# The opening of a two-block transformer kernel: input in two transfers, a split of the first weights by VectorE, and another order of the first products

## What is computed

```
mod_l = (silu(c) @ ada_w[0] + ada_b[0])          # shifts, scales and gates
h_l = rms_norm(x_lat, norm1_g[0]) * (1 + s1_l) + sh1_l
h_c = rms_norm(x_ctx, norm1_g[0]) * (1 + s1_c) + sh1_c
h = concatenate([h_c, h_l], axis=1)
proj = h @ w_in                                   # q, k, v, r
q, k, v, r = split(proj, [512, 1024, 2048])
q, k = rope_2d(q), rope_2d(k)                     # on the latent tokens
...
```

## Time and profile before

| | |
|---|---|
| median of three runs | 2332.44 us |
| the profiled execution | 2329.71 us, span 2327.6 us |
| TensorE busy | 1946.0 us, 84% of the span |
| VectorE, ScalarE, GpSimd busy | 930.4, 687.7 and 93.8 us |
| DMA | 592.29 MB, mean 254 GB/s |
| mean granted TensorE clock | 0.938 |

### The profile page before, as it was taken

The page is one execution under the profiler, slowest core; times in us unless marked ns, Lnnn a source line. Parts: engine busy times, 40 slices in busy tenths (PEclk is TensorE's granted clock), DMA queues, the critical chain, the costliest instruction groups (busy, mean ns, idle before and its releaser), DMA issues.

```text
span 2327.6 us, 38292 instructions
## 1 busy us (share of the span) xinstructions
PE 1946.0 (84%) x16711; PEld 1467.0 (63%) x16711; DVE 930.4 (40%) x1634; ACT 687.7 (30%) x1253; POOL 93.8 (4%) x112
## 2 busy tenths in 40 slices
PE   6998899999999999999998999666666576666666
PEld 4996667888788887999896476433333343333433
DVE  4446745433524246665666365333111121111111
ACT  4334435222424246554553322111111011111111
POOL 0011110000001011000200000000000000000000
PEclk9999999999999999999999999888888888888889
DMA  6316553221225224444530359999999999999997
GB/s 277 145 37 274 199 226 131 78 109 53 97 96 217 109 74 173 177 165 150 217 121 10 157 207 397 426 427 427 427 427 427 427 426 427 427 427 427 428 427 311
DMA packets 48007, 592.29 MB, mean 254 GB/s; under 512 B 5934, under 2 KB 6890, under 8 KB 12001
## 3 DMA queue, kind: packets, MB, share of 16 engines
q1 hardware_dynamic: 44416, 580.21, 60.8%
q0 software_dynamic: 2992, 8.57, 1.2%
q10 hardware_dynamic: 432, 1.06, 0.1%
HBM read 588.77 MB, written 1.05 MB: 253 GB/s over the span
## 4 chain that ended last, share of the span: by engine, by line
PE 47%; DMA 29%; DVE 6%; ACT 4%; issue 2%; POOL 0%; SPq 0%; DVEq 0%; ACTq 0%; POOLq 0%
DMA s_ring<-in_w_up 14%; PE bank L725 10%; PE bank L727 10%; PE bank L726 10%; DMA s_arena<-in_w_up 6%; PE bank L1458 5%; DMA s_xT<-in_w_up 4%; DMA s_hT<-in_w_up 3%; DVE s_ring_r L2416 2%; ACT s_arena_r L1694 2%; PE bank L1494 2%; DMA s_xT<-in_w_down 1%; PE bank L1445 1%; PE bank L1277 1%; PE bank L1500 1%
## 5 line engine op out<-in xcount | busy, mean ns | idle before, releaser
L725 PE MATMUL bank<-s_arena_r 128*128 128x256 f32 (+2 forms) x1858 | 603.9, 325 | 8.5 <-DVE s_hT_r L2421 3.9
L727 PE MATMUL bank<-s_arena_r,s_ring_r 128*128 128x256 f32 (+2 forms) x1514 | 499.7, 330 | 0.0
L1694 ACT ACTIVATE s_arena<-bank 32x256 f32<-32x256 f32 (+6 forms) x418 | 167.9, 407 | 1001.7 <-PE bank L1458 536.9
L1458 PE MATMUL bank<-s_ring,s_arena 128*32 128x256 f32 x1952 | 281.0, 506 | 143.2 <-DMA s_hT<-in_w_up 40.3
L726 PE MATMUL bank<-s_hT_r,s_arena_r 128*128 128x512 f32 (+2 forms) x1200 | 399.3, 333 | 0.0
L725 PEld LDWEIGHTS bank<-s_arena_r 128*128 128x128 f32 x1858 | 347.9, 187 | 46.0 <-issue 8.9
L2416 DVE TENSOR_TENSOR s_ring_r<-s_ring,s_arena_r 128x2048 fp32r<-128x2048 f32 (+3 forms) x120 | 247.8, 2077 | 273.7 <-ACT s_arena_r L1694 273.6
L727 PEld LDWEIGHTS bank<-s_arena_r,s_ring_r 128*128 128x128 f32 x1514 | 284.8, 188 | 28.8
L1458 PEld LDWEIGHTS bank<-s_ring,s_arena 128*32 128x32 f32 x1952 | 136.0, 144 | 218.4 <-issue 205.8
L1694 ACT ACTIVATE s_arena_r<-s_ring 128x2048 fp32r<-128x2048 f32 (+3 forms) x120 | 206.2, 1730 | 153.5 <-PE bank L727 123.6
L726 PEld LDWEIGHTS bank<-s_hT_r,s_arena_r 128*128 128x128 f32 x1200 | 225.3, 188 | 24.1 <-issue 0.5
(11 more groups left out here) (398 smaller groups left out, 2505.2 us busy)
## 6 DMA issues: line engine op xcount, KB each, us to landing
s_ring<-in_slabs SPq DMA_DIRECT2D x68, 2048.0 KB, 8.3
s_ring<-in_w_down SPq DMA_DIRECT2D x32, 2048.0 KB, 28.9
s_ring<-in_w_up SPq DMA_DIRECT2D x31, 2048.0 KB, 33.7
s_ring<-in_w_gate SPq DMA_DIRECT2D x30, 2048.0 KB, 33.2
s_arena<-in_w_gate SPq DMA_DIRECT2D x16, 2048.0 KB, 33.5
s_arena<-in_w_up SPq DMA_DIRECT2D x16, 2048.0 KB, 33.2
s_arena<-in_w_down SPq DMA_DIRECT2D x14, 2048.0 KB, 28.8
s_ring<-in_slabs SPq DMA_DIRECT2D x16, 1408.0 KB, 6.1
```

The lines of the kernel that those rows point to most:

```text
L725: mm(out, w_hi_, x_hi_, start=start, stop=False, skip_group_check=skip)
L727: return mm(out, w_lo_, x_hi_, start=False, stop=stop, skip_group_check=skip)
L1458: last = mm(pb[b][32 * q:32 * q + 32, 0:256], x[:, c, :], (gate, up)[q // 2](c, q % 2), start=c == 0, stop=c == DC - 1, skip_group_check=True)
L1694: return act.activation(out, in_, func, **kw)
```

## The change

Six edits, all in the opening.

1. SP fetches `xT` in two transfers of four chunks. The first signals `early_in`, the second `xT_in`. `ka` now signals `early_in` too, and both TensorE (before `ada_rows(0)`) and ACT (before the first squares) wait for `early_in` at 32, that is for the first half of `xT` and for `ka`. ACT waits for `xT_in` before chunk 4.
2. GpSimd waits until `w_lo` is 1. It then rounds all of quarter 1, and after it only chunks 4 to 7 of quarter 0.
3. VectorE rounds chunks 0 to 3 of quarter 0 itself and takes their rest (`first_w_in(0, 0, 4)`). Its order is now: factors 0 to 5, columns, factors 6 and 7, rest of chunk 0, this half quarter, rests of chunks 1 and 2, quarter 1, rest of chunk 3, second half of quarter 0, columns.
4. TensorE starts with units 0 and 1 on chunks 0 to 2, then `ada_rows(2)`, chunk 3 of both, `ada_turn(2)`, unit 2 on chunks 0 to 3, `ada_rows(3)`, unit 3 on chunks 0 and 1, `ada_turn(3)`, unit 3 on chunks 2 and 3, and then chunks 4 to 7 of units 0 to 3 interleaved. The RoPE products come two by two behind units 4 to 6.
5. ACT rounds quarter 2 before it drains unit 0 rather than after unit 1.
6. `w_lo` counts one more step, so its later thresholds rise by one.

```diff
--- before.py
+++ after.py
@@ -34,8 +34,8 @@
 NE, NG, EPG = 64, 8, 8
 DE = 512
 
-W_GLA, W_FFN, W_NA = 19, FC + DC, 17
-W_GLA_OUT = 13
+W_GLA, W_FFN, W_NA = 20, FC + DC, 17
+W_GLA_OUT = 14
 W_NA_OUT = W_GLA + W_FFN + 11
 A_NA_W = 16
 H_AT = [0 * DC, 2 * DC, 3 * DC, 5 * DC, 6 * DC]
@@ -520,7 +520,8 @@
 
         @block.sync
         def _(sp):
-            sp.dma_start(xT[:, :, :], d["xT"].rearrange("p (c t) -> p c t", t=TT)).then_inc(S["xT_in"], 16)
+            for c0, sem in ((0, "early_in"), (DC // 2, "xT_in")):
+                sp.dma_start(xT[:, c0:c0 + DC // 2, :], d["xT"].rearrange("p (c t) -> p c t", t=TT)[:, c0:c0 + DC // 2, :]).then_inc(S[sem], 16)
             for n in range(len(slabs)):
                 if free[n]:
                     sp.wait_ge(S[free[n][0]], free[n][1])
@@ -620,9 +621,9 @@
             pool.memset(one1[:, :], 1.0).then_inc(S["ones_set"], 1)
             pool.memset(ada_sc, 0.0).then_inc(S["pool_set"], 1)
             pool.memset(eps[:, :], EPS).then_inc(S["ones_set"], 1)
-            pool.wait_ge(S[landed[gla_at[0]][0]], landed[gla_at[0]][1])
-            for k in range(2):
-                pool.tensor_copy(g_w_hi[k], half(place[gla_at[0]], k)).then_inc(S["pool_set"], 1)
+            pool.wait_ge(S["w_lo"], 1)
+            for k, c0 in ((1, 0), (0, DC // 2)):
+                pool.tensor_copy(g_w_hi[k][:, c0:DC, :], half(place[gla_at[0]], k)[:, c0:DC, :]).then_inc(S["pool_set"], 1)
             for hd in range(8):
                 h, p = hd // 2, hd % 2
                 for i, (x, y) in enumerate(((g_e3[:, two(h, p), :], g_qk[:, h, :]), (g_tm[:, p, :], g_qk[:, 4 + h, :]))):
@@ -853,7 +854,7 @@
             pe.wait_ge(S["sq_used"], DC - 1)
             mm(pb[7][:, :], ON[1024], g_tm[:, 0, :], start=True, stop=False)
             norm_chunk("n1_0", DC - 1, DC, 7, TT, 1024)
-            pe.wait_ge(S["ka_in"], 16)
+            pe.wait_ge(S["early_in"], 32)
             pe.wait_ge(S["sc_ready"], 1)
             ada_rows(0)
             ada_rows(1)
@@ -869,40 +870,49 @@
             def unit(u, chunks):
                 k = u // 2
                 wh, wl, o = g_w_hi[k % 2], half(place_r[gla_at[k // 2]], k % 2), 128 * (u % 2)
-                pe.wait_ge(S["w_lo"], k + (1 if k < 2 else 2))
+                pe.wait_ge(S["w_lo"], k + (1 if k < 2 else 3))
                 if u >= 4:
                     pe.wait_ge(S["gla_qk_ev"], u - 3)
                 for c in chunks:
                     if u == 0:
                         pe.wait_ge(S["h_lo"], c + 1)
+                        if c == DC // 2:
+                            pe.wait_ge(S["w_lo"], 3)
                     last = split_mm(pb[u % 4][:, :], wh[:, c, o:o + 128], wl[:, c, o:o + 128], g_h_hi[:, c, :], hT_r[:, c, :], c == 0, c == DC - 1)
                 return last
+
+            def pair(u, chunks):
+                for c in chunks:
+                    for x in (u, u + 1):
+                        last = unit(x, [c])
+                        if c == DC - 1:
+                            last.then_inc(S["gla_qk_mm"], 1)
+            pair(0, range(3))
             ada_rows(2)
-            for c in range(2):
-                unit(0, [c])
-                unit(1, [c])
+            pair(0, [3])
+            ada_turn(2)
+            unit(2, range(4))
             ada_rows(3)
-            unit(0, [2])
-            unit(1, [2])
-            ada_turn(2)
-            unit(0, [3])
-            unit(1, [3])
+            unit(3, range(2))
             ada_turn(3)
-            unit(2, range(4))
-            unit(3, range(4))
-            for u in range(8):
-                unit(u, range(4 if u < 4 else 0, DC)).then_inc(S["gla_qk_mm"], 1)
-                if u == 0:
-                    pe.wait_ge(S["gla_in"], 64)
-                if u >= 1:
-                    rope_turn(u - 1)
+            unit(3, range(2, 4))
+            pair(0, [4, 5])
+            unit(2, [4, 5])
+            pair(0, [6, 7])
+            unit(3, [4, 5])
+            pair(2, [6, 7])
+            pe.wait_ge(S["gla_in"], 64)
+            for u in range(4, 8):
+                unit(u, range(DC)).then_inc(S["gla_qk_mm"], 1)
+                for v in range(2 * u - 8, min(2 * u - 6, 7)):
+                    rope_turn(v)
             rope_turn(7)
             pe.wait_ge(S["gla_qk_ev"], 8)
 
             def token_major(k, name, freed, after, first=0):
 
                 wh, wl = g_w_hi[k % 2 + (2 if k >= 8 else 0)], half(place_r[gla_at[k // 2]], k % 2)
-                pe.wait_ge(S["w_lo"], k + 2)
+                pe.wait_ge(S["w_lo"], k + 3)
                 for u in range(4):
                     if freed:
                         pe.wait_ge(S[freed[0]], freed[1] + u + 1)
@@ -1693,7 +1703,7 @@
                     tables(TABLE_OF[func])
                 return act.activation(out, in_, func, **kw)
             act.dma_start(cols[:, :], d["cols"]).then_inc(S["cols_in"], 16)
-            act.dma_start(ka[:, :], d["k_a"]).then_inc(S["ka_in"], 16)
+            act.dma_start(ka[:, :], d["k_a"]).then_inc(S["early_in"], 16)
             tables(ACT.Silu)
             act.wait_ge(S["cols_in"], 16)
             act.wait_ge(S["pool_set"], 1)
@@ -1849,8 +1859,11 @@
                     A(f_t1[:, i % 4, 0:T], f_t1[:, i % 4, 0:T], ACT.Silu).then_inc(S["ffn_silu"], 1)
                 ffn_out_prepared(l, T)
 
+            act.wait_ge(S["early_in"], 32)
+            squares("n1_0", DC // 2, lambda c: xT[:, c, :])
             act.wait_ge(S["xT_in"], 16)
-            squares("n1_0", DC, lambda c: xT[:, c, :])
+            for c in range(DC // 2, DC):
+                square(norms["n1_0"][0], c, xT[:, c, :])
             root_factor("n1_0", DC, 7, TT)
 
             def gla_w_in_hi(k):
@@ -1868,9 +1881,10 @@
                 modulate(0, 0, TT, 4 * part, 4 * part + 4)
             act.wait_ge(S["gla_in"], 64)
             A(g_aw1_hi, g_aw1, ACT.Copy).then_inc(S["w_hi"], 1)
+            gla_w_in_hi(2)
             for u in range(8):
                 copy("gla_qk_mm", u + 1, "gla_qk_ev", pb[u % 4][:, :], g_qk[:, u, :], scale=128.0 ** -0.5 if u < 4 else 1.0)
-                if u % 2:
+                if u % 2 and u > 1:
                     gla_w_in_hi(u // 2 + 2)
             gla_w_in_hi(6)
             for u in range(4):
@@ -2504,11 +2518,17 @@
 
             def gla_w_in_lo(k):
                 w, w_r, hi = half(place[gla_at[k // 2]], k % 2), half(place_r[gla_at[k // 2]], k % 2), g_w_hi[k % 2 + (2 if k >= 8 else 0)]
-                if k < 2:
-                    dve.wait_ge(S["pool_set"], k + 2)
-                    TTn(w_r, w, hi.bitcast(F32), ALU.subtract).then_inc(S["w_lo"], 1)
+                w_rest(w, w_r, hi)
+
+            def first_w_in(k, c0, c1):
+
+                w, w_r, hi = [x[:, c0:c1, :] for x in (half(place[gla_at[0]], k), half(place_r[gla_at[0]], k), g_w_hi[k])]
+                if c1 < DC:
+                    dve.wait_ge(S[landed[gla_at[0]][0]], landed[gla_at[0]][1])
+                    step(dve.tensor_copy(hi, w))
                 else:
-                    w_rest(w, w_r, hi)
+                    dve.wait_ge(S["pool_set"], 3 - k)
+                TTn(w_r, w, hi.bitcast(F32), ALU.subtract).then_inc(S["w_lo"], 1)
 
             def factors(c0, n):
                 for c in range(c0, c0 + n):
@@ -2525,16 +2545,16 @@
             rsq("n1_0", TT)
             factors(0, 6)
             columns(0)
-            gla_w_in_lo(0)
-            rest(0)
-            rest(1)
-            factors(6, 1)
-            rest(2)
-            factors(7, 1)
-            rest(3)
+            factors(6, 2)
             dve.wait_ge(S["mod_xr"], DC)
             dve.sem_inc(S["norm_done"], 1)
-            gla_w_in_lo(1)
+            rest(0)
+            first_w_in(0, 0, DC // 2)
+            rest(1)
+            rest(2)
+            first_w_in(1, 0, DC)
+            rest(3)
+            first_w_in(0, DC // 2, DC)
             columns(1)
             for c in range(4, DC):
                 rest(c)
```

## The result

The changed kernel takes 2337.35 us (median of 21 runs, 2333.74 to 2340.62) against 2331.5 us for the kernel before in as many (one of these took 3730.81 us, which does not move the median). The ratio is 1.002, interval 1.0014 to 1.0025: slower by some 5 us, at the bound of 0.2% that I had set for "no change". The range of the prediction (2331.5 to 2337.5) holds the time, at its upper end; the forecast, +2.6 us, was half of what came. The two medians lie 5.85 us apart. The forecast was laid on 2332.44 us, the median of the three runs known then. As a difference its range ended at +5.1 us, between the 4.7 us of the ratio and the 5.85 us of the medians: that it holds the time is partly luck.

What follows compares the result with a forecast made beforehand. Taken as bound by TensorE work, then from 1454.30 us by expert-weight landings with DMA saturated. Start -0.2, low clock +0.1 and order +2.7 gave +2.6 us on 2332.44: 2335.0 us, 8-in-10 range 2331.5 to 2337.5.

Steps and rivals of the forecast that it cites:

- The shared semaphore: Input transfers: `ka` lands with the second half of `xT`, the split buys nothing, the squares start 0.3 us later.
- VectorE's half quarter and GpSimd's hold: Opening: TensorE starts at 30.5 us, 0.2 us earlier; GpSimd's later copies cost 0, at most 0.3 us.
- The waits behind the last turn: TensorE's new order after `ada_turn(3)`: waits for chunks 4, 5 and quarter 2, with rounding +2.7 us.
- The low clock in the opening: TensorE's opening: the clock still rises at about 33.7 us, so an earlier start loses 0.1 us more.
- the second rival: Opening: the low clock lasts twice as long, 1.5 us more lost; 2336.5 us, 2337.5 with upper bounds; chance 0.15.
- Reaches the end undiminished.: Whole kernel: a microsecond lost or won in the opening reaches the end, as saturated DMA starts from released buffers.
- the two signs of being wrong: Last turn comes before 44 us, or the difference at the v columns is not that at the end.

Runs made afterwards that it cites:

- e12_idle5: The changed kernel plus five products nobody reads in TensorE's gap behind the second turn; 2334.52 us (one run), kernel before beside it 2332.51.
- e7_later_idle: The changed kernel plus three short products in each of three later gaps (220, 250, 280 us); 2330.87 us, ratio 0.9991 to the kernel before.
- e10_before_filled: The kernel before plus three short products in each of three later gaps (220, 250, 280 us); 2328.56 us, ratio 0.998.
- e1_old_order: The changed kernel with the old TensorE order and ScalarE rounding quarter 2 after unit 1 again; 2333.93 us, ratio 1.0006 to the kernel before.
- e8_before_look: The kernel before, unchanged, run again for a second profile; 2330.25 us (one run), kernel before beside it 2332.52.
- e9_plan_filled: e6_new_plan with five unread products instead of four, plus the short products of e7_later_idle; 2323.24 us, ratio 0.9964 to the kernel before.
- e4_idle: The changed kernel plus two products nobody reads in TensorE's gap behind the second turn; 2336.27 us, ratio 1.0018 to the kernel before.
- e5_idle4: The changed kernel plus four products nobody reads in TensorE's gap behind the second turn; 2335.46 us, ratio 1.0015 to the kernel before.
- e6_new_plan: The changed kernel with `ka` on its own semaphore, four unread products behind the second turn and another TensorE order; 2328.52 us, ratio 0.9986 to the kernel before.

## Why the prediction was right in kind and short in size

**The shared semaphore.** Right: `ka` keeps step with the second half and the split buys nothing; the squares came 0.56 us later, against 0.3 forecast and 0.6 as the bound. The Trainium skill, "DMA: Bandwidth & Descriptors", section on queues, rings and completion order, lets an engine drain a packet of typically 9 to 17 descriptors before it goes to the next ring. By that `ka` would have been early. The changed kernel disagrees: `ka` landed 8.8 us after its issue, with the second half of `xT`.

**VectorE's half quarter and GpSimd's hold.** Right: gain in 0.17 us, rounding in 0.69 (0.75 taken), start at 30.60 (30.5), and no wait of TensorE for the rests of chunks 1 to 3. The last holds at the low clock only: in e12_idle5 they cost 0.5 us.

**The waits behind the last turn.** Right in place and number: three waits, for chunk 4, chunk 5 and quarter 2, idle for 1.63, 0.90 and 0.35 us against 1.5 to 1.6, 1.1 and 0.4 forecast. The term was mis-sized, +2.7 against +3.3, because I compared unlike things. A row's idle time begins at the modelled end of a product, 0.39 us behind its start, while products follow each other every 0.23 us. The new waits cost 2.02 + 1.30 + 0.74 - 3 x 0.23 = 3.4 us of pace. The wait of the kernel before, which I put at 0.48 us from the row of its weight load, cost 0.44 - 0.23 = 0.2 and 0.1 at the restart. The difference is 3.3 with the restarts' due, not 2.7.

**The low clock in the opening.** The step "+0.1 us" failed: I let the clock rise at 33.7 us in the changed kernel because it did so in the kernel before. It rose at 36.0 us in the first profile and at 33.9 in the second; the loss there was 2.6 and 1.7 us against 1.4 before (the second rival, which I gave 0.15, in part). So the last turn ended at 47.4 us and not at 46.3. Sum for the first profile: -0.1 + 1.15 + 3.3 = 4.35 us.

**"Reaches the end undiminished."** This failed too, on the side that I had not looked at. I asked whether a delay is swallowed; here it grew, from 4.35 us at the v columns to 6.7 at the end, which is one of the two signs of being wrong that I had named. Behind the v columns the changed kernel lost 1.6 and 3.9 us more by 290 us in its two profiles, through a clock that falls in gaps of some 2 us which the kernel before has as well, and passes partly at the full clock. e7_later_idle and e10_before_filled show that: fill the gaps, and the difference no longer grows between the v columns and 290 us. I had read the granted clock for the opening only. The rows for 200 to 295 us with their gaps of 2.0 to 2.3 us would have told that a shift by a few microseconds is a throw of dice there, worth about 1.6 us for each low stretch of 3.4 us; my range should have reached some 3 us higher.

**What stays open.** What decides behind which of these gaps the clock falls. The kernel before showed the same two stretches in two profiles and in e10_before_filled none at 206 and 222 us either; e1_old_order, whose v columns come within 0.04 us of it, fell at 201 and 221 us. And the loss grew by another 1 us between 1454 us and the end in the changed kernel's profile, part of it in the last weight transfer (30.69 us against 30.08), which I did not pursue. One profile says little of it: from 1454 us on, two profiles of the same kernel (before and e8_before_look) lie up to 2 us apart and end within 0.9 us of each other. Nor is it known why the kernel before alone has the idle time near 206 us.

## What to carry to other kernels

When an order is written out by hand, put the producers that start a long chain (here the last slab's rows and its turn) early enough that independent work at least as long as the chain stands behind them: 5.5 us covered it in the old order, 1.4 us did not. A count shared by two transfers makes each waiter wait for both. And before pricing a change of a few microseconds, look for gaps of TensorE all along the kernel behind which the clock may or may not fall; a few products that nobody reads were worth as much here (4 us in the kernel before) as the best opening of these runs gains by the v columns (4.1 us in e9_plan_filled).

## What the runs showed of the hardware that I had not expected

- In e4_idle a float32 product of 128x512 (two passes in the rows) took 1.84 us at 16.6 us and 0.94 us at 24.9 us, in windows whose rows both give the granted clock as 1.00. So TensorE ran at the low clock at the start of the program, though the rows show 1.00 there. When it first rises differs between profiles of one opening and moves the start of the units by up to 0.6 us: in e7_later_idle the norm's last product was already faster (1.54 us against 1.92 for its two passes) and the first slab's 128 products took 3.70 us; in the changed kernel's first profile these took 4.66.
- The granted clock fell behind a gap of 1.85 us (e5_idle4) and 1.97 us (e6_new_plan) and did not behind 1.04 us (e12_idle5) or 0.54 us (e9_plan_filled); nor did it behind 2.01 us at 219 us in the kernel before.
- Every low stretch up to 300 us lasted 3.4 or 6.8 us in all fourteen profiles.
